# A modulation vector's last eight row chunks, summed by VectorE instead of TensorE

## The chip, the cores and the metric

The kernel runs on one core of a Trainium2 chip. The metric is the device time of one execution in microseconds, lower is better; the times given are medians of several runs. TensorE (PE in the profile) multiplies matrices, VectorE (DVE), ScalarE (ACT) and GpSimd (POOL) work element by element, and SyncE (SP) issues nearly all DMA transfers from one queue.

## The reference

Two transformer-like blocks on 256 tokens of width 2048, all in fp32. What the change touches is the modulation of the first block, and what stands around it:

```python
c_act = jax.nn.silu(c)                          # 1 x 2048
mod = c_act @ w_ada[l] + b_ada[l]               # 2048 x (6 * 2048)
sh1, sc1, gt1, sh2, sc2, gt2 = jnp.split(mod[:, None, :], N_MOD, axis=-1)
h = _rmsnorm(x, norm1_g[l]) * (1.0 + sc1) + sh1
p = h @ w_in[l]
y_rwkv = _rwkv7_mixer(p[..., :N_RWKV_COLS], ...)   # a recurrence over tokens, 16 heads
y_pool = _pool_mixer(p[..., N_RWKV_COLS:], ...)
mix = jnp.concatenate([y_rwkv, y_pool], axis=-1) @ w_out[l]
x = x + gt1 * mix
h = _rmsnorm(x, norm2_g[l]) * (1.0 + sc2) + sh2    # first use of sc2, the fifth vector
x = x + gt2 * _conv_ffn(h, w_up[l], ...)
```

The second block (convolution, windowed attention, gates, another FFN) follows and is not touched.

## The kernel before

**Weights.** All weights stream from HBM in chunks of 1 MB (128 x 2048 fp32) through `raw`, a ring of four slots that SyncE fills strictly in the order `ORDER`, each time when the slot's last reader has signalled (`freed`). A weight chunk ("w") has two halves of 128 x 1024. ScalarE writes a rounded copy `whi` of a half (`cut_hi`, line 1312), VectorE the rest `wlo` (`cut_lo`, line 1773), and TensorE multiplies both with the activations (lines 651 and 652: 128x512 and 128x256). "lead" is the cut of a half some steps ahead of its product; `lo_ready` counts cut halves, `half_used` multiplied ones.

**Modulation.** The six vectors are rows of the product c_act x w_ada. A chunk of w_ada ("ada") is 128 rows by 2048 columns of one vector, 16 chunks to a vector. `ada_chunk` (line 700) multiplies the uncut chunk with `crep`, a column of c_act repeated 32 times, in four column groups that add up in the PSUM bank `ada`; at the end of a vector ScalarE copies the bank to `ada_row` (`copy_ada`, line 1378), TensorE turns it into columns (`ada_turn`, line 709), and VectorE adds the bias into `mod` (`mod_columns`, line 1864). Before, five vectors (`PE_VECTORS`, 80 chunks) go this way: 32 chunks at the start, 6 in the opening segment, and 14 in each of the segments 1 to 3 (`SEGMENT_ADA`), two at each even step below 14. The sixth vector is summed by VectorE row chunk by row chunk in the later up1 stage (`late_row`, line 2221, one instruction for a half of 128 x 1024), and `ada_late` (line 716) sums the 128 partitions with a matrix of ones.

**Segments.** The recurrence of group g (four of them) runs in segment g+1, in 16 steps, mixed by hand with products. In segments 1 to 3 the products are those of the next group's projections; in the last segment (s = 4, here called the last) they are the first half of w_out ("woutp"), one tile of eight pairs of matmuls for each step, in two quarters. `recurrence_step` gives TensorE's small products of a step in two parts: steps 1 to 6 invert matrices (`z_step` line 878, `t_step` lines 891 and 897), steps 7 to 12 pass the state through four chunks (`u_step` 947, `s_step` 958, `r_step` 924, `y_step` 971), step 13 takes the variance (`var_step` 1005) and step 14 spreads it (`var_spread` 1011). Between them lie VectorE's and ScalarE's parts (`recurrence`, lines 1979 to 2049). VectorE's order in a step n of the last segment is: `r_out` in steps 8 and 11, the cut of half n+2, the residual tile of step n-1 (line 2163, two instructions of 128x256), the recurrence part, and at n = 13 `mixed_low` (line 2152). After step 15 it runs

```python
            for s in range(SEGMENTS):
                segment(s)
                if s == SEGMENTS - 1:
                    norm_scale(1, 4, 5, "norm2_g")
            dve.wait_ge(mixed, NGROUP)
            mixed_low(6, 2, NR + 6)
```

and four more cuts. Then comes the stage wout: TensorE's `first_four` makes tiles 0 to 3 in four parts of eight pairs; its parts 0, 1, 2 and 3 each wait for one cut half (those cut in steps 14 and 15 and the first two of the four), and parts 2 and 3 also for `mixed_low(6, 2)`. Twelve tiles of one half each follow, and their residual tiles. A tile of woutp needs the residual tile of three tiles before, one of wout that of four before. The stage ends with the norm of x1, then up1 begins.

**Buffers.** `mix[:, NR:KT]` (the pool mixer's output) is read for the last time in step 0 of the last segment, and `aa` in segment 3.

## Time and profile before

| | us |
|---|---|
| median of 3 runs | 2660.87 |
| lowest, highest | 2657.83, 2666.80 |
| the profiled execution | 2657.71 |
| its span (first to last instruction) | 2655.5 |
| PE busy in the span | 2594.1 |
| DVE busy | 1875.0 |
| ACT busy | 1279.5 |
| DMA moved | 554.86 MB |

Segments 1, 2 and 3 stand at about 213.6, 289.3 and 365.0 us from the start of the span, the last segment at 441.2, the stage wout at 516.0, up1 at 568. A busy PE counts as busy when any matmul is in flight; a wait of an engine stands in brackets behind the instruction that ended it, with the engine, tile and line that released it. Successive instructions of an engine overlap by some hundredths of a microsecond, so that the distance of two starts is a little less than the duration.

### The profile page before, as it was taken

The page shows a single profiled execution, that of the slowest core. Times are in us where ns is not written, and L with a number is a line of the kernel's source. Part 1 is how long each engine was busy: PE and PEld are TensorE (multiplying, and loading weights), DVE is VectorE, ACT ScalarE, POOL GpSimd, SP SyncE. Part 2 cuts the span into 40 slices and gives each one's busy share as a digit, 9 for nine tenths or more (in the row PEclk, how much of TensorE's full clock was granted, in tenths as well). Part 3 has the DMA queues.
Part 4 walks back from the last instruction along what each step waited for, and adds up shares of the span by engine and source line. Part 5 has one row for each costly group of instructions (what it writes and reads, how often), then busy time and mean ns, then how long its engine had stood idle before and what let it go on. Part 6 is the DMA issues. An engine that isn't in the chain of part 4 may idle for free.

```text
span 2655.5 us, 48131 instructions
## 1 busy us (share of the span) xinstructions
PE 2594.1 (98%) x17668; PEld 2176.3 (82%) x17668; DVE 1875.0 (71%) x2718; ACT 1279.5 (48%) x1800; POOL 149.8 (6%) x150
## 2 busy tenths in 40 slices
PE   5999999999999999999999999999999999999998
PEld 1677776888888888888888888888888888888887
DVE  1475666778888887555577877787688888885554
ACT  2354443355555555444433465554455555554443
POOL 1311111020000000000000000001100000000000
PEclk8999999999999999999999999999999999999999
DMA  9957775346666655555555544455555555555553
GB/s 375 381 228 268 290 277 206 139 160 236 237 237 237 237 197 184 205 201 210 199 189 178 188 159 158 160 182 195 190 177 190 189 189 189 190 190 206 205 200 132
DMA packets 86806, 554.86 MB, mean 209 GB/s; under 512 B 8496, under 2 KB 8624, under 8 KB 24496
## 3 DMA queue, kind: packets, MB, share of 16 engines
q1 hardware_dynamic: 86272, 551.78, 56.5%
q8 instruction: 74, 1.21, 0.2%
q10 hardware_dynamic: 432, 1.64, 0.2%
q14 instruction: 28, 0.23, 0.0%
HBM read 551.29 MB, written 2.10 MB: 208 GB/s over the span
## 4 chain that ended last, share of the span: by engine, by line
PE 87%; DVE 6%; DMA 3%; issue 2%; ACT 2%; DVEq 0%; SPq 0%; ACTq 0%
PE bank L651 38%; PE bank L652 19%; PE banks L651 15%; PE banks L652 8%; DMA raw<-in_stream_dram 3%; DVE wlo L1773 2%; PE bank L700 1%; DVE yb L2468 0%; DVE yb L2471 0%; ACT whi L1312 0%; PE banks L878 0%; PE banks L1245 0%; PE banks L1265 0%; PE banks L897 0%; PE banks L1105 0%
## 5 line engine op out<-in xcount | busy, mean ns | idle before, releaser
L1773 DVE TENSOR_TENSOR wlo<-raw,whi 128x1024 fp32r<-128x1024 f32 x846 | 1031.0, 1228 | 213.5 <-ACT whi L1312 209.4
L1312 ACT ACTIVATE whi<-raw 128x1024 fp32r<-128x1024 f32 x846 | 878.4, 1052 | 424.2 <-PE bank L652 325.0
L651 PE MATMUL bank<-act,whi 128*128 128x512 f32 x2928 | 1045.4, 399 | 1.4 <-DVE act L2152 0.9
L652 PE MATMUL bank<-act,wlo 128*128 128x256 f32 x2928 | 819.6, 280 | 0.0
L651 PEld LDWEIGHTS bank<-act,whi 128*128 128x128 f32 x2928 | 548.7, 187 | 146.3 <-issue 18.4
L651 PE MATMUL banks<-act,whi 128*128 128x512 f32 x1792 | 633.9, 396 | 7.9 <-DVE act L1823 6.8
L652 PEld LDWEIGHTS bank<-act,wlo 128*128 128x128 f32 x2928 | 553.2, 189 | 1.0 <-issue 0.7
L652 PE MATMUL banks<-act,wlo 128*128 128x256 f32 x1792 | 504.7, 282 | 0.0
L651 PE MATMUL bank<-ff,whi 128*128 128x512 f32 x1408 | 493.3, 393 | 1.0 <-DVE wlo L1773 1.0
L651 PEld LDWEIGHTS banks<-act,whi 128*128 128x128 f32 x1792 | 338.6, 189 | 91.1 <-issue 13.5
L652 PE MATMUL bank<-ff,wlo 128*128 128x256 f32 x1408 | 392.9, 279 | 0.0
L652 PEld LDWEIGHTS banks<-act,wlo 128*128 128x128 f32 x1792 | 341.8, 191 | 0.0
L651 PEld LDWEIGHTS bank<-ff,whi 128*128 128x128 f32 x1408 | 263.8, 187 | 64.4 <-DVE wlo L1773 1.7
L1599 ACT ACTIVATE yb<-joined,par 128x256 f32<-128x256 f32 x176 | 105.9, 603 | 346.9 <-DVE joined L1793 181.4
L652 PEld LDWEIGHTS bank<-ff,wlo 128*128 128x128 f32 x1408 | 263.8, 187 | 0.0
L2210 DVE SCALAR_TENSOR_TENSOR yb<-joined,par,yb 128x255 f32<-128x255 f32 x352 | 169.1, 481 | 24.7 <-DVE yb L2210 5.5
L2518 POOL TENSOR_TENSOR ssq<-ssq,ft 128x256 f32<-128x256 f32 x75 | 71.0, 947 | 1364.3 <-ACT ft L1585 1345.5
L700 PE MATMUL bank<-raw,crep 128*32 128x512 f32 x640 | 90.1, 665 | 28.8 <-DMA raw<-in_stream_dram 28.8
L651 PE MATMUL bank<-gated,whi 128*128 128x512 f32 x256 | 89.7, 393 | 0.4 <-DVE yb L2468 0.4
L1585 ACT ACTIVATE ft<-x 128x256 f32 (+1 forms) x64 | 26.6, 415 | 106.4 <-DVE x L2162 86.1
L2162 DVE TENSOR_TENSOR x<-bank,x 128x256 f32 (+1 forms) x64 | 27.2, 424 | 70.3 <-PE bank L652 69.2
L700 PEld LDWEIGHTS bank<-raw,crep 128*32 128x32 f32 x640 | 15.6, 113 | 71.6 <-DMA raw<-in_stream_dram 42.9
(281 smaller groups left out, 1943.2 us busy)
## 6 DMA issues: line engine op xcount, KB each, us to landing
raw<-in_stream_dram SPq DMA_DIRECT2D x503, 1024.0 KB, 4.8
late_in<-in_stream_dram SPq DMA_DIRECT2D x16, 1024.0 KB, 6.7
x<-in_x_dram SPq DMA_DIRECT2D x1, 2048.0 KB, 13.6
lora_w<-in_lora_dram SPq DMA_DIRECT2D x1, 1536.0 KB, 12.3
pool_w<-in_pool_w_dram SPq DMA_DIRECT2D x1, 1024.0 KB, 12.1
out_dram<-x SPq DMA_DIRECT2D x2, 512.0 KB, 2.8
out_dram<-x ACTq DMA_DIRECT2D x2, 512.0 KB, 3.0
catt<-in_att_dram ACTq DMA_DIRECT2D x1, 576.0 KB, 3.2
```

What stands on the lines that cost most here:

```text
L651: nc.tensor.matmul(tile_bank(t), wh, flat(pair[:, kt]), start=starts and n == 0, stop=False)
L652: mm = nc.tensor.matmul(small_half(t), wl, pair[:, kt, 0], start=False, stop=stops and last)
L700: mm = nc.tensor.matmul(ada[32 * g:32 * g + 32, :], crep[:, kt], src[:, 512 * g:512 * g + 512], start=kt == 0, stop=kt == KT - 1, tile_pos ...
L1312: nc.scalar.activation(whi[:, k % RING], raw[:, r % RING, 8 * (k % 2):8 * (k % 2) + 8], ACT.Copy)\
L1585: nc.scalar.activation(ft[:, j % 2], one(x, j + 4 * i), ACT.Square).then_inc(sq_ready, 1)
L1599: nc.scalar.activation(yb[:, j], joined[:, j % 2], ACT.Identity, scale=pcol(conv, 3 * j + tap + 12 * i), bias=pcol(bias, j + 4 * i)).then_ ...
L1773: nc.vector.tensor_tensor(wlo[:, k % RING], raw[:, r % RING, 8 * (k % 2):8 * (k % 2) + 8], whi[:, k % RING].bitcast(F32), ALU.subtract).th ...
L2162: return nc.vector.tensor_tensor(dst, half, dst, ALU.add)
L2210: ins = nc.vector.scalar_tensor_tensor(out=yb[:, j, dst], in0=joined[:, j % 2, src], scalar=pcol(conv, 3 * j + tap + 12 * i), in1=yb[:, j, ...
L2518: nc.gpsimd.tensor_tensor(ssq[:], ssq[:], ft[:, q], ALU.add).then_inc(ssq_ready, 1)
```

## The change

Chunks 8 to 15 of the fifth vector (sc2, `VECTORS` index 4) leave TensorE's list: segments 1 and 2 have 12 ada chunks each (none at step 12), segment 3 has 10 (none at steps 10 and 12). The ring has eight entries fewer. The eight chunks come in 16 halves of 512 KB, issued by SyncE between the loads of the last segment into `mix[:, NR:KT]`, two halves at a time; half o waits until VectorE has done half o-2. VectorE scales and adds one half at the end of each of the steps 2 to 15 of the last segment, and the last two in wout at tiles 4 and 5, into `aa`. TensorE sums the partitions at wout's tile 8 (`ada_late`), ScalarE copies before tile 10, TensorE turns at tile 11, and VectorE adds the result to the half vector already in `mod` at tile 12, where `norm_scale` now stands too. ScalarE's copies of the fourth and fifth vectors are at steps 2 and 10 of segment 3 instead of step 12 of segment 2 and step 14 of segment 3.

```diff
-SEGMENT_ADA = 14
+SEGMENT_ADA = {1: 12, 2: 12, 3: 10}
+SEGMENT_FIRST = {1: 38, 2: 50, 3: 62}
+ROWS = 8
+PE_CHUNKS = PE_VECTORS * KT - ROWS
+ROW_STEP = 2
-VECTORS = (1, 0, 2, 3, 4, 5)
+VECTORS = (1, 0, 2, 3, 4, 4, 5)
...
+        row_in = mix[:, NR:KT].rearrange("p (g k) t -> p g (k t)", g=2)
+        row_sum = aa[:].rearrange("p (g k) t -> p g (k t)", g=2)
...
+            def load_row_half(o):
+                q, g = o // 2, o % 2
+                if o == 0:
+                    sp.wait_ge(a_ready, 16 * FILLS.index("mixed") + NR)
+                if o >= 2:
+                    sp.wait_ge(row_added, o - 1)
+                src = stream[KT * 4 + KT - ROWS + q, :, HALF * g:HALF * g + HALF]
+                sp.dma_start(row_in[:, g], src).then_inc(row_full[g], 16)
...
+                behind = n - FIRST_CHUNK["woutp"] - RING
+                if what == "w" and 0 <= behind < ROWS:
+                    load_row_half(2 * behind)
+                    load_row_half(2 * behind + 1)
...
             for n in range(4, TILES["wout"]):
+                if n == 8:
+                    pe.wait_ge(row_added, 2 * ROWS)
+                    pe.wait_ge(tile_sum, FIRST_TILE["wout"])
+                    ada_late(row_sum)
+                if n == 11:
+                    pe.wait_ge(gn_out, NGROUP)
+                    ada_turn(PE_VECTORS)
...
-                    if (s, n) in ((1, 10), (2, 12), (3, 14)):
-                        copy_ada(1 + s)
+                    if (s, n) in ((1, 10), (3, 2), (3, 10)):
+                        copy_ada({(1, 10): 2, (3, 2): 3, (3, 10): 4}[s, n])
...
+                if n == 10:
+                    copy_ada(PE_VECTORS)
...
+            def row_part(o):
+                q, g = o // 2, o % 2
+                dve.wait_ge(row_full[g], 16 * (q + 1))
+                activation = crep[:, KT - ROWS + q, 0:1]
+                if q == 0:
+                    nc.vector.tensor_scalar(row_sum[:, g], row_in[:, g], activation, None, ALU.mult).then_inc(row_added, 1)
+                else:
+                    dve.wait_ge(row_added, o - 1)
+                    nc.vector.scalar_tensor_tensor(out=row_sum[:, g], in0=row_in[:, g], scalar=activation, in1=row_sum[:, g],
+                                                   op0=ALU.mult, op1=ALU.add).then_inc(row_added, 1)
...
-                    elif n == 13:
-                        dve.wait_ge(mixed, NGROUP - 1)
-                        mixed_low(0, 6, NR)
+                    else:
+                        if n == 13:
+                            dve.wait_ge(mixed, NGROUP - 1)
+                            mixed_low(0, 6, NR)
+                        if n >= ROW_STEP:
+                            row_part(n - ROW_STEP)
...
                 segment(s)
-                if s == SEGMENTS - 1:
-                    norm_scale(1, 4, 5, "norm2_g")
...
                 lead("wout", n, 0, 0)
+                if n in (4, 5):
+                    row_part(2 * ROWS - 6 + n)
                 done("wout", n, 0, 0)
                 residual_tile("wout", n, 0, 2)
+                if n == 12:
+                    mod_added(PE_VECTORS)
+                    norm_scale(1, 4, PE_VECTORS + 1, "norm2_g")
```

## Rows read from the trace of the kernel before

**Rows 1.** The page, busy time of each engine in the span.
```profile
PE 2594.1 (98%) x17668; PEld 2176.3 (82%) x17668; DVE 1875.0 (71%) x2718; ACT 1279.5 (48%) x1800; POOL 149.8 (6%) x150
```
**Rows 2.** Busy by stretch: length, busy PE PEld DVE ACT POOL (count), PEclk, DMA share, GB/s.
```profile
365.00:441.20 76.20, 74.90 (x1175) 53.84 (x1174) 48.16 (x85) 31.02 (x53) 8.70 (x6) 1.00 0.72 277
...
458.00:516.00 58.00, 58.00 (x824) 47.57 (x817) 37.65 (x67) 22.70 (x36) 4.11 (x4) 1.00 0.33 111
516.00:528.40 12.40, 11.30 (x67) 9.64 (x65) 8.95 (x14) 4.58 (x6) 0.00 (x0) 1.00 0.67 246
528.40:562.60 34.20, 34.17 (x192) 29.41 (x192) 26.93 (x40) 17.66 (x27) 16.91 (x15) 1.00 0.46 157
```
**Rows 3.** Timeline of PE, end of segment 1: start us, us, instruction, [wait].
```profile
275.63 1.92 PE L700 MATMUL bank<-raw,crep 128*32 128x512 f32 x16
...
283.63 0.66 PE L1011 MATMUL bank<-res,zmat 128*128 128x128 f32 x4 [0.80 <-DVE zmat L2040]
```
**Rows 4.** Timelines of ACT and of DVE in the same stretch.
```profile
277.60 0.63 ACT L1461 ACTIVATE zmat<-t 128x512 f32<-128x512 f32 x1 [6.29 <-DVE t L2035]
278.13 2.18 ACT L1312 ACTIVATE whi<-raw 128x1024 fp32r<-128x1024 f32 x2
...
279.21 2.36 DVE L1773 TENSOR_TENSOR wlo<-raw,whi 128x1024 fp32r<-128x1024 f32 x2 [1.65 <-ACT whi L1312]
...
283.15 0.43 DVE L2040 COPY zmat<-small 128x512 f32<-128x512 f32 x1
```
**Rows 5.** Timelines of PE and of DVE, segment 3, step 10.
```profile
417.72 1.92 PE L700 MATMUL bank<-raw,crep 128*32 128x512 f32 x16
419.58 0.27 PE L958 MATMUL banks<-tok 64*64 64x64 f32 x2
...
417.47 0.41 DVE L2008 COPY us<-banks 64x256 f32<-64x256 f32 x1
420.31 0.48 DVE L2019 SCALAR_TENSOR_TENSOR state<-banks,dc,wssq 128x64 f32<-128x64 f32 x2 [2.43 <-PE banks L958]
```
**Rows 6.** Timeline of ACT, segment 3, step 2; durations of line 1378 (min/median/max ns).
```profile
377.77 0.60 ACT L1440 ACTIVATE tinvt<-banks 128x512 f32<-128x512 f32 x1 [4.95 <-PE banks L891]
...
L1378 ACT ACTIVATE ada_row<-bank x6: 577/590/598, 53.8 to 1061.0; 128x512 f32<-128x512 f32 x6
```
**Rows 7.** Durations (min/median/max ns) of two VectorE lines.
```profile
L2221 DVE SCALAR_TENSOR_TENSOR late_sum<-late_in,crep,late_sum x32: 1276/1280/1281, 619.8 to 958.0; 128x1024 f32<-128x1024 f32 x32
...
L1932 DVE TENSOR_SCALAR yb<-kraw,par x4: 346/353/353, 170.6 to 397.6; 128x256 f32<-128x256 f32 x4
```
**Rows 8.** Timelines of DVE and of PE, last segment, step 9.
```profile
488.99 1.23 DVE L1773 TENSOR_TENSOR wlo<-raw,whi 128x1024 fp32r<-128x1024 f32 x1
490.25 1.00 DVE L2163 SCALAR_TENSOR_TENSOR x<-bank,mod,x 128x256 f32<-128x256 f32 x2
491.17 0.47 DVE L2019 SCALAR_TENSOR_TENSOR state<-banks,dc,wssq 128x64 f32<-128x64 f32 x2
...
491.98 0.34 PE L924 MATMUL banks<-state,ar 64*64 64x64 f32 x8
```
**Rows 9.** Timeline of DVE, from the last segment into wout.
```profile
519.36 4.80 DVE L1773 TENSOR_TENSOR wlo<-raw,whi 128x1024 fp32r<-128x1024 f32 x4
527.33 3.74 DVE L2163 SCALAR_TENSOR_TENSOR x<-banks,mod,x 128x256 f32<-128x256 f32 x8 [3.17 <-PE banks L652]
```
**Rows 10.** Timeline of PE, the turn of the fifth vector.
```profile
461.76 0.60 PE L709 MATMUL bank<-res,ada_row 128*128 128x128 f32 x4
```
**Rows 11.** Timeline of PE at step 1 of the last segment; busy in the stretch behind it.
```profile
453.19 0.69 PE L878 MATMUL banks<-tinvt,bm 64*64 64x64 f32 x32 [2.57 <-DVE tinvt L1995]
...
453.20:458.00 4.80, 4.80 (x104) 4.02 (x104) 3.30 (x5) 1.63 (x2) 1.04 (x1) 0.64 0.23 93
```
**Rows 12.** DMA issues: KB each, median us from issue to landing.
```profile
late_in<-in_stream_dram SPq DMA_DIRECT2D x16, 1024.0 KB, 6.7
...
cw<-in_wkv_dram SPq DMA_DIRECT2D x1, 480.0 KB, 13.9
```

More of the change, by code:

```diff
@@ L74 @@
 OPEN_ADA = {6: 2, 8: 2, 10: 2}
-SEGMENT_ADA = 14
+SEGMENT_ADA = {1: 12, 2: 12, 3: 10}
+SEGMENT_FIRST = {1: 38, 2: 50, 3: 62}
 PE_VECTORS = 5
-LATE = 5
+ROWS = 8
+PE_CHUNKS = PE_VECTORS * KT - ROWS
+ROW_STEP = 2
+LATE = 6
 LATE_FIRST, LATE_END = 2, 2 + KT
@@ L97, in raw_order @@
                 c += 1
-            for _ in range(OPEN_ADA.get(n, 0) if s == 0 else 2 - 2 * (n % 2) if n < SEGMENT_ADA else 0):
+            for _ in range(OPEN_ADA.get(n, 0) if s == 0 else 2 - 2 * (n % 2) if n < SEGMENT_ADA.get(s, 0) else 0):
                 order.append(("ada", a))
                 a += 1
-    assert a == PE_VECTORS * KT
+    assert a == PE_CHUNKS
     return order + [("w", m) for m in range(c, N_WEIGHT_CHUNKS)]
@@ L400, in blocks_program @@
         late_full, late_added = sem("late_full"), sem("late_added")
+        row_full, row_added = [sem(f"row_full{g}") for g in range(2)], sem("row_added")
         sq_ready, ssq_ready, stat_ready, std_ready = sem("sq_ready"), sem("ssq_ready"), sem("stat_ready"), sem("std_ready")
@@ L700, in ada_chunk @@
                     mm = nc.tensor.matmul(ada[32 * g:32 * g + 32, :], crep[:, kt], src[:, 512 * g:512 * g + 512],
-                                          start=kt == 0, stop=kt == KT - 1, tile_position=(0, 32 * g))
+                                          start=kt == 0, stop=kt == KT - 1 or n == PE_CHUNKS - 1, tile_position=(0, 32 * g))
                 mm.then_inc(ada_used, 1)
@@ L710, in ada_turn, with ada_late @@
                 mm.then_inc(ada_turned, 1)
-            def ada_late():
-                pe.wait_ge(late_added, 2 * KT + 2)
+            def ada_late(total):
                 for g in range(4):
                     mm = nc.tensor.matmul(ada[32 * g:32 * g + 32, :], ones[:, 0:32],
-                                          late_sum[:, g // 2, 512 * (g % 2):512 * (g % 2) + 512], start=True, stop=True,
+                                          total[:, g // 2, 512 * (g % 2):512 * (g % 2) + 512], start=True, stop=True,
                                           tile_position=(0, 32 * g))
@@ L1147, in segment @@
                             quarter(s, q)
-                        if part == 1 and n % 2 == 0 and n < SEGMENT_ADA and not last:
+                        if part == 1 and n % 2 == 0 and n < SEGMENT_ADA.get(s, 0):
                             for a in (n, n + 1):
-                                ada_chunk(ADA0 + sum(OPEN_ADA.values()) + SEGMENT_ADA * (s - 1) + a)
+                                ada_chunk(SEGMENT_FIRST[s] + a)
                         if not last:
@@ L1201, in _ @@
             loop("up1", 4, LATE_END, None, LATE_FIRST)
-            ada_late()
+            pe.wait_ge(late_added, 2 * KT + 2)
+            ada_late(late_sum)
             loop("up1", 4, 22, None, LATE_END)
@@ L1372, in copy_ada @@
             def copy_ada(n):
-                act.wait_ge(ada_used, KT * (n + 1) if n < PE_VECTORS else KT * PE_VECTORS + 1)
+                act.wait_ge(ada_used, KT * (n + 1) if n < PE_VECTORS - 1 else PE_CHUNKS + n - PE_VECTORS + 1)
                 if n:
@@ L1864, in mod_columns, with mod_added @@
                 nc.vector.tensor_tensor(dst, src, bias, ALU.add).then_inc(mod_ready, 1)
+            def mod_added(n):
+                dve.wait_ge(ada_turned, n + 1)
+                dve.wait_ge(mod_ready, n)
+                src = aux[:, :].rearrange("p (b g r) -> p g b r", b=4, g=4)[:, :, :, 0]
+                dst = mod[:, VECTORS[n]].rearrange("p (g b) -> p g b", g=4)
+                nc.vector.tensor_tensor(dst, src, dst, ALU.add).then_inc(mod_ready, 1)
+            def row_part(o):
[8 more added lines that the diff above has]
+                                                   op0=ALU.mult, op1=ALU.add).then_inc(row_added, 1)
             def norm_scale(n, which, ready, name):
@@ L2335, in _ @@
             mod_columns(LATE)
-            dve.wait_ge(mod_ready, 6)
+            dve.wait_ge(mod_ready, LATE + 1)
             dve.wait_ge(derived, 6)
```

## The prediction

> **What bounds the kernel now.** I read the page first. TensorE is busy for 98% of the span, VectorE for 71% [rows 1]. So time can come back only where TensorE does less, and only if nothing else was the last to finish there. Then I took the busy time by stretch, because that share is an average over stages [rows 2]. In segment 3 TensorE works 74.90 of 76.20 us. In steps 2 to 14 of the last segment it works 58.00 of 58.00, while VectorE works 37.65 and has 20.35 us free. At the step into wout (516.0 to 528.4) VectorE has 3.4 us free, nearly all of it one wait of 3.17 us at the end [rows 9]. The reader should see that VectorE's free time in the last segment is about as large as the work that the change puts there, and that it lies in pieces between things TensorE waits for. The timelines of these places give the rest.
>
> **What TensorE gives up.** A pair of ada chunks takes 1.92 us, and the next instruction starts 1.86 us behind its start [rows 3, 5]. Four pairs go: 7.4 us of TensorE time. What each is worth is read at its place.
>
> *Step 12 of segments 1, 2 and 3 (three pairs).* At the end of segment 1 TensorE waits 0.80 us for VectorE's zmat, at 283.63 [rows 3]. I follow that wait back [rows 4]: zmat 283.15, which needed ScalarE's square root, which stands on ScalarE behind a tile that VectorE joined after two cuts (279.21, 2.36 us), which waited for ScalarE's cuts (278.13), which stand behind the square at 277.60, which waited for VectorE's y_out. VectorE came to y_out through its own queue. No link is the pair at 275.63. Without the pair TensorE reaches its next quarter 1.86 us sooner and then waits: about 0.9 us in front of the variance products (the square ends at 278.23) and 1.65 us at 283.63 in place of 0.80. Worth zero, three times over. The bound on the other side is the full 3 x 1.86 = 5.6 us.
>
> *Step 10 of segment 3 (one pair).* Here the pair is on the path [rows 5]. VectorE's u_out ends at 417.88, the state products could start at 417.95 and start at 419.58, and VectorE waits 2.43 us for them. All that follows up to the last segment hangs on them. Worth 1.63 us.
>
> *The copies that move.* The first chunk of the fifth vector waits for the fourth vector's copy (0.59 us), now at step 2 of segment 3. ScalarE has been idle 4.95 us before its instruction at 377.77 [rows 6], so the copy is done by about 373.5. TensorE comes to that chunk at 378.1. It costs nothing. If that cover were gone it would cost 0.6. Later weight chunks only arrive sooner, with eight chunks fewer ahead of them.
>
> **What VectorE takes on.** The sixth vector's rows are the same instruction on the same shape: 1.28 us [rows 7]. Successive starts lie closer than durations: four cuts of 1.22 us take 4.80 [rows 9]. I take 1.20 for a part and keep 1.28 as upper bound. The two first parts are TENSOR_SCALAR, 0.35 us at a quarter of the size [rows 7]; four of them (1.4) bound one from above, 0.7 is my value. Both fall in steps where VectorE has over 2 us free, so it doesn't matter. I lay the parts into VectorE's order, step by step, with its durations of before, and let each instruction start when its engine and its releaser allow. Without the parts this hand replay gives the starts of before within 0.1 us. Clock times below are those of before, with no shift for segment 3.
>
> 1. Steps 2 to 8: VectorE is caught up each time before TensorE needs it. Nothing.
> 2. Step 9 [rows 8]: before, the cut starts at 488.99 and the state output at 491.17, and TensorE's r products at 491.98. A part of 1.20 now stands in front of the cut, and the state output ends at 492.84. TensorE starts at 492.89: 0.94 us late.
> 3. Step 10: the part of step 9, cut (1.20), residual (0.92) and u_out end at 497.31. TensorE, already 0.94 late, waits 0.38 more.
> 4. Step 12: the same queue makes y_out end at 507.30 and the square at 507.97. TensorE waits 0.35 more.
> 5. Steps 13 to 16: `mixed_low` (1.67), the part, a cut, a residual tile, the group's scaling, then 1.1 us on ScalarE, two finishing operations, the part of step 14, and only then the cut that `first_four`'s part 1 needs: done at 521.89, wanted at 520.49. 1.45 late.
> 6. Residual tile, the part of step 15, residual tile, `mixed_low(6, 2)` and the next cut end at 526.78. `first_four`'s part 2 wants it at 524.75. 2.08 late. Before, this cut was the first of the four that began at 519.36 [rows 9], ready 1.1 us ahead.
>
> Sum of waits: 0.94 + 0.38 + 0.35 + 1.45 + 2.08 = 5.20 us. The 3.17 us in which VectorE waited afterwards [rows 9] don't help, as they lie behind the wait. The last two parts, in wout, are hidden: VectorE has 7.3 us free there [rows 2], and tile 8 needs the sum only after about 10 us.
>
> **What TensorE takes on.** `ada_late` for the rows is one group of eight, half a pair: 0.93 us. The extra turn is 0.60 us, 0.53 from start to start [rows 10]. Both stand in wout, where TensorE is busy 34.17 of 34.20 us [rows 2], so both count: 1.46 us. The copy (0.59), the bias-like addition and the moved `norm_scale` (0.17 each) have most of a tile (2.8 us) to spare.
>
> **Transfers.** Half o is issued when half o-2 has been added, two steps (about 9 us) ahead of its use. The nearest row is late_in: 1 MB lands in 6.7 us [rows 12], and these are 512 KB, with DMA busy 0.33 there [rows 2]. Hidden. SyncE's waits hold back the weights queued behind them: chunk 5+b of the last segment is issued at the end of step 2b+1 and first cut at step 2b+7. Also hidden.
>
> **Sum.** -1.63 + 5.20 + 0.93 + 0.53 = +5.0 us. With 1.28 for a part the waits grow to 5.76 and the sum is +5.6. With 0.80, far below any such row, it is +2.5. With the three other pairs worth all of their 5.6 us it would be -0.6. Against the profiled execution (2657.71, span 2655.5) this is 2662.7. That execution lies 3.2 us under the median of the runs shown, so against the median it is 2665.9. I predict 2666. A measurement of this kernel tells a change from none at about 0.3%, 8 us: this reads as no change, a little on the slow side.
>
> **Rivals.**
>
> *Everything comes back.* VectorE's order leaves room for the parts and the three pairs of step 12 are worth their time: -7.4 + 1.46 = -5.9, 2655. For it speaks 20.35 us of free time for 14 parts of 1.20 [rows 2]. Against it, the chain in rows 4, in which TensorE has no part. Even this stays inside 8 us. Chance 0.06, half of it with something on top.
>
> *The parts fit, the pairs don't pay.* -1.63 + 1.46 = -0.2, 2660.7. This needs VectorE to be off the path at steps 9 to 16. Chance 0.09.
>
> *The clock falls (slower).* Behind a wait of 2.57 us in step 1 of the last segment TensorE's granted clock is 0.64 on average over 4.80 us, so it fell to its lower level (1.2 GHz) for part of it: 4.80 x 0.36 = 1.7 us lost [rows 11]. The change makes such places: 1.45 and 2.08 us close together at wout's start, and 0.9 and 1.65 us at each of three segment ends. One fall makes +6.7, four make 5.0 + 6.9 = +11.9, 2673. From two falls on it decides against "no change". For it: the waits are many, and 2.57 was enough. Against it: each is shorter than 2.57, and the wait of 1.10 us at 528.39, the same kind, was followed by a clock of 1.00 [rows 2]. Chance 0.19 for two or more.
> The Trainium skill, TensorE: Matmul & The Clock Gate, section "A second HAM failure mode: psum-queue depth-cycling", says that frequent short idles between groups of matmuls can make the clock swing between its levels. By that rule the time would be nearer the +11.9 of this rival; by the clock of 1.00 behind the single short wait it stays at the sum.
>
> *Row halves land late (slower).* If a half took 13.9 us like the small transfer in rows 12, then the two steps of 9.1 us would stretch by 4.8, six times: +29 on top. That one was issued with larger ones around it. It decides from landings of about 9 us. Chance 0.04.
>
> **How the numbers follow.** The forecast, +2.5 to +8 and thus 2663 to 2669, has 0.62. The range must hold the rivals down to the pairs' price and up to four falls, and the spread of the runs shown (2657.8 to 2666.8), so 2657 to 2673. Faster by over 0.3%: 0.03. Slower by over 0.3%: the clock 0.18, late halves 0.04 and 0.02 of the forecast's upper edge, 0.24. Within: 0.73.
>
> **What would show each step.** In the changed profile: (a) at the ends of segments 1 to 3 the wait at line 1011 is about 1.65 us, with another near 0.9 in front of line 1005, and segments 1 and 2 are as long as before (75.7 us). Shorter ones make the zero wrong. (b) Segment 3 is 1.6 us shorter. (c) TensorE waits for VectorE's state at steps 9 and 10, and twice within `first_four`, 1.5 and 2.1 us. If VectorE shows idle time in steps 9 to 16 other than for ScalarE's 1.1 us, my order is wrong. (d) The parts last 1.28 us and wait for no DMA. (e) Granted clock of 1.00 from 516 to 562. (f) From 441 to the norm of x1, 6.7 us more than before. The forecast fails if (e) shows 0.9 or less, or if the waits in (c) are absent.

## The result and the profile after

The changed kernel takes 2669.15 us in the median of 18 runs (2664.63 to 2673.71), the kernel before 2660.26 in 18 runs beside them (2654.83 to 2666.8). The ratio is 1.003, 95% interval 1.0022 to 1.0038: slower by 8 us (5.9 to 10.1), just at the bound of what I had called no change, inside the range and 3 us above the forecast. The profiled execution of after is the slowest of its 18 runs (2673.71, 4.6 above the median) and that of before was 2.5 below its own. So the two traces differ by 15.6 us of span where the medians differ by 8.9, and what is read from them must be split into what the program does and what an execution draws. The sections below do that.

The page of the changed kernel, busy time by engine. Against [rows 1] VectorE's sum is 17.6 us up, as it should be; TensorE's is 7.3 up too, though it has four pairs less: its work took longer somewhere.

```profile
span 2671.1 us, 48070 instructions
PE 2601.4 (97%) x17616; PEld 2176.5 (81%) x17616; DVE 1892.6 (71%) x2735; ACT 1278.5 (48%) x1801; POOL 150.7 (6%) x150
```

The waits of TensorE in the changed kernel from 170 to 600 us: line, releaser, sum in us, times, longest.

```profile
PE bank L1026 <- ACT zmat L1491: 3.2, 4, 1.0
PE bank L1032 <- DVE zmat L2092: 2.9, 3, 1.4
PE banks L899 <- DVE tinvt L2047: 2.5, 1, 2.5
PE banks L673 <- DVE wlo L1805: 2.4, 2, 1.7
...
PE banks L899 <- issue: 1.7, 1, 1.7
...
PE banks L945 <- DVE state L2071: 1.6, 4, 1.1
```

**The pairs of step 12.** The timeline of TensorE at the end of segment 1, where [rows 3] stood before. The pair is gone; TensorE comes to the variance products early and waits 0.97 us, then waits 1.40 in place of 0.80:

```profile
278.00 1.05 PE L1026 MATMUL bank<-res,zmat 128*128 128x2 f32 x8 [0.97 <-ACT zmat L1491]
...
283.33 0.66 PE L1032 MATMUL bank<-res,zmat 128*128 128x128 f32 x4 [1.40 <-DVE zmat L2092]
```

Segment 1's products begin 0.26 us earlier than before and those of segment 3 0.14 earlier: two pairs of 1.86 us went out of segments 1 and 2 and nothing came back.

**The pair of step 10 of segment 3.** The product ahead of it (L968, 420.06) is 3.30 late, for a reason that follows. The state products start at 421.48, 1.90 after those of before [rows 5], so 1.40 us came back; for 0.39 of the rest TensorE waits for VectorE:

```profile
420.06 0.45 PE L968 MATMUL banks<-rs,tinv 64*64 64x64 f32 x8
...
421.48 0.27 PE L979 MATMUL banks<-tok 64*64 64x64 f32 x2 [0.39 <-DVE us L2060]
```

**A stall that nobody forecast.** In step 4 of segment 3 the 32 small products of the inverse break off after 17. The timeline of TensorE, and the busy time around it (columns as in [rows 2]):

```profile
390.71 0.50 PE L899 MATMUL banks<-tinvt,bm 64*64 64x64 f32 x17
...
392.88 0.46 PE L899 MATMUL banks<-tinvt,bm 64*64 64x64 f32 x15 [1.67 <-issue]
```

```profile
386.00:391.00 5.00, 5.00 (x121) 3.05 (x112) 1.06 (x3) 2.10 (x4) 2.79 (x2) 1.00 0.59 221
391.00:394.00 3.00, 1.33 (x31) 1.08 (x24) 0.60 (x1) 0.00 (x0) 0.00 (x0) 0.93 0.89 322
394.00:397.00 3.00, 3.00 (x50) 2.37 (x52) 1.22 (x2) 0.97 (x1) 0.00 (x0) 0.50 0.88 369
397.00:400.00 3.00, 3.00 (x73) 2.46 (x69) 2.00 (x3) 1.77 (x5) 0.00 (x0) 1.00 0.20 27
```

"Issue" means that no semaphore released the instruction. TensorE stands 1.67 us in the middle of a group that waits for nothing, and behind it the granted clock is 0.50 (the 1.2 GHz level) for 3 us. Together 3.4 us: the work before it is 0.14 us ahead of before's, the work behind it 3.30 late. In before all of 391 to 397 is busy at a clock of 1.00. The low clock is this execution's: the profiles of runs 1, 2, 4, 7 and 8 have nine more such idles of 0.21 to 1.80 us, and behind none of them does the clock fall.

**The last segment and wout.** TensorE's timeline at step 9, step 10, the variance products and the two parts of `first_four`, where [rows 8, 9] stood:

```profile
495.26 0.34 PE L945 MATMUL banks<-state,ar 64*64 64x64 f32 x8 [1.11 <-DVE state L2071]
...
499.88 0.27 PE L979 MATMUL banks<-tok 64*64 64x64 f32 x2 [0.47 <-DVE us L2060]
...
510.59 1.05 PE L1026 MATMUL bank<-res,zmat 128*128 128x2 f32 x8 [0.27 <-ACT zmat L1491]
...
524.18 0.51 PE L673 MATMUL banks<-act,whi 128*128 128x512 f32 x1 [0.74 <-DVE wlo L1805]
...
528.93 0.50 PE L673 MATMUL banks<-act,whi 128*128 128x512 f32 x1 [1.66 <-DVE wlo L1805]
```

Five waits at the five forecast places, for the forecast releasers, 4.25 us in all. The wait of 1.10 us at wout's fifth tile (528.39 in the kernel before) is in both kernels and not among them. The parts and the transfers of the row halves (duration in ns min/median/max, first and last start):

```profile
L588 SPq DMA_DIRECT2D mix<-in_stream_dram x16: 327/328/435, 447.5 to 526.3; - x16
L1915 DVE SCALAR_TENSOR_TENSOR aa<-mix,crep,aa x12: 1274/1277/1286, 473.1 to 525.0; 128x1024 f32<-128x1024 f32 x12
L1912 DVE TENSOR_SCALAR aa<-mix,crep x2: 743/744/746, 462.8 to 468.3; 128x1024 f32<-128x1024 f32 x2
...
DMA to landing us min/median/max: 3.5/4.4/6.4
```

### The profile page after: what moved, and what is told of

It reads as the page before. It is cut to its first block, busy times and chain, and to the rows that moved or that the text cites. A ratio compares the mean times of both kernels' runs of the same rounds, so it can differ in the third digit from the quotient of the medians.

```text
span 2671.1 us, 48070 instructions
## 1 busy us (share of the span) xinstructions
PE 2601.4 (97%) x17616; PEld 2176.5 (81%) x17616; DVE 1892.6 (71%) x2735; ACT 1278.5 (48%) x1801; POOL 150.7 (6%) x150
## 4 chain that ended last, share of the span: by engine, by line
PE 87%; DVE 7%; DMA 3%; issue 2%; ACT 1%; DVEq 0%; SPq 0%; ACTq 0%
PE bank L673 38%; PE bank L674 19%; PE banks L673 16%; PE banks L674 8%; DMA raw<-in_stream_dram 3%; DVE wlo L1805 2%; PE bank L722 2%; DVE yb L2526 0%; DVE yb L2529 0%; PE banks L899 0%; ACT whi L1342 0%; DVE aa L1915 0%; DVE x L2218 0%; PE banks L1275 0%; PE banks L1295 0%
## 5 line engine op out<-in xcount | busy, mean ns | idle before, releaser
L722 PE MATMUL bank<-raw,crep 128*32 128x512 f32 x576 | 83.3, 679 | 26.9 <-DMA raw<-in_stream_dram 26.9
L1822 DVE TENSOR_REDUCE joined<-banks 128x256 f32<-128x512 f32 x50 | 34.3, 691 | 56.7 <-PE banks L674 56.6
```

What stands on the lines that cost most here:

```text
L722: mm = nc.tensor.matmul(ada[32 * g:32 * g + 32, :], crep[:, kt], src[:, 512 * g:512 * g + 512], start=kt == 0, stop=kt == KT - 1 or n == P ...
L1822: nc.vector.tensor_reduce(dst, halves, AX.X, ALU.add).then_inc(tile_sum, 1)
```

## The experiments

All are timed in five rounds beside the kernel before. "Late" and "early" below are starts of the same instruction against the kernel before, counted from segment 1's products, so that the start of an execution, which varies by some 2 us, is left out. One thing in these offsets is not of the programs: the clock behind the wait in step 1 of the last segment fell in the kernel before [rows 11], which cost it 1.5 us, and whether it falls there differs between executions of one program (last section).

**1. The removal alone.** The changed kernel without row transfers, parts, late sum and turn: 72 chunks on TensorE, so half of the fifth vector is missing from the sum.

```
-                    load_row_half(2 * behind)
-                    load_row_half(2 * behind + 1)
...
-                    pe.wait_ge(row_added, 2 * ROWS)
...
-                    ada_late(row_sum)
...
-                    ada_turn(PE_VECTORS)
...
-                        if n >= ROW_STEP:
-                            row_part(n - ROW_STEP)
...
-                    mod_added(PE_VECTORS)
```

> Leaves the last eight chunks of the fifth vector out altogether (no transfers, no parts, no late sum, no second turn), so sc2 lacks half of its sum. My theory: only the pair at step 10 of segment 3 was on TensorE's path, so the time is 1.4 to 1.6 us under the kernel before, unless the stall of 3.3 us that the changed kernel's profile shows in step 4 of segment 3 (1.67 us with no releaser, then a low clock) belongs to the shorter TensorE program: then it is 1.7 us over it, and the stall is in this profile too. Rival (everything comes back): 7.4 us under it, with no wait at lines 1005 and 1011 beyond the old 0.80 us.

2661.76, ratio 1.0006 (0.9993 to 1.002). Four pairs, 7.4 us of TensorE's work, are gone and the kernel isn't faster. Segments 1 and 2 are as long as before; step 10 gives 1.4; and the same 17 and 15 split is there, with a second one in step 5:

```profile
392.85 0.46 PE L898 MATMUL banks<-tinvt,bm 64*64 64x64 f32 x15 [1.41 <-issue]
...
400.03 0.27 PE L898 MATMUL banks<-tinvt,bm 64*64 64x64 f32 x2 [1.80 <-issue]
```

They cost 3.75 us, so segment 3 ends 2.3 us late. Step 1 of the last segment gives back 1.5 of that, because the clock stayed at 1.00 there, and the stage wout 0.6. The norm of x1 is 0.2 late. By the program the stalls took more than the pairs gave. The stall therefore doesn't come from the parts or their transfers.

**2. The parts cut to 16 columns.** All transfers, waits and the late sum stay; only VectorE's time goes; the sum leaves out the other columns.

```
-  nc.vector.scalar_tensor_tensor(out=row_sum[:, g], in0=row_in[:, g], ...
+  nc.vector.scalar_tensor_tensor(out=row_sum[:, g, 0:16], in0=row_in[:, g, 0:16], ...
```

> The changed kernel with all its transfers, waits and TensorE work, but each part of VectorE works on 16 columns in place of 1024 (sc2 lacks the rest). My theory: the four waits of TensorE for VectorE's queue (1.1, 0.5, 0.3 in steps 9 to 13 and 0.7 and 1.7 at wout's start, some 4.3 us) go, and the time falls by 4 to 5 us from the changed kernel. Rival (late transfers or the SyncE queue hold things up): the waits stay. Rival (the loss lies outside these stages): it falls by less than 2 us. The TensorE program is that of the changed kernel, so a stall in step 4 of segment 3 that comes from its length shows here again; one that comes by chance most likely does not.

2665.01, 1.0017 (1.0003 to 1.0031). The five waits are gone; the stall (1.68, and a second one of 1.00 in step 5, 3.2 us lost with the clock at 1.00) and the late sum with its turn remain; the norm of x1 is 2.9 late. The transfers as such cost nothing.

**3. The parts alone.** The kernel before plus the 16 transfers and the 16 parts, whose sum is not used; TensorE's program is that of before.

```
+                if what == "w" and 0 <= behind < ROWS:
+                    load_row_half(2 * behind)
+                    load_row_half(2 * behind + 1)
...
+                        if n >= ROW_STEP:
+                            row_part(n - ROW_STEP)
```

> The kernel before with only the 16 transfers of 512 KB and VectorE's 16 parts added at the places of the change; TensorE still multiplies all 80 chunks and the sum of the parts is not used. My theory: 4.5 to 5.8 us over the kernel before, all of it in steps 9 to 13 and at wout's start. Rival (VectorE's free time holds them): within 1 us of it. If a slower up1 loop comes with the parts' transfers or code, it shows here as more than 6 us; if it comes with the TensorE program, this one has the loop of before (22.19 us an iteration).

2663.12, 1.002 (1.0005 to 1.0035). TensorE's waits from 440 to 570 us in this kernel:

```profile
PE banks L670 <- DVE wlo L1792: 3.0, 3, 1.9
...
PE banks L943 <- DVE state L2050: 1.1, 1, 1.1
...
PE banks L977 <- DVE us L2039: 0.5, 1, 0.5
PE bank L1024 <- ACT zmat L1480: 0.2, 1, 0.2
```

4.8 us of waits, the norm of x1 6.5 late, and no stall in segment 3. This is the parts' cost by itself. The lateness grows by more than each wait: by 1.19, 0.88, 0.51, 1.07, 2.20 and 0.56 us at waits of 1.12, 0.45, 0.25, 0.74, 1.93 and 0.35.

**4. The changed kernel again.**

> The changed kernel again, for a second profile. If the 3.3 us stall in step 4 of segment 3 and the up1 loop of 22.61 us an iteration (22.19 before) are properties of its program, both stand here again, and the time is 8 to 9 us over the kernel before. If they vary from execution to execution, the stall is elsewhere or absent and the loop differs, while the waits in steps 9 to 13 and at wout's start stand within 0.1 us.

2670.52, 1.0034 (1.002 to 1.0047). Stall of 1.68 at the same instruction, waits 0.27, 0.74 and 1.71, the norm of x1 8.3 late (9.3 in the first profile). The first profile shows one stall and a low clock behind it; this one shows two stalls and a clock of 1.00 from 391 to 400, and loses 2.9 us there in place of 3.4:

```profile
398.09 0.27 PE L899 MATMUL banks<-tinvt,bm 64*64 64x64 f32 x2 [0.72 <-issue]
```

**5. Other pairs.** Which pair is dropped should matter more than how many. The parts stay; the pairs of steps 2, 4, 6 and 10 of segment 3 go, those of step 12 come back, and ScalarE's copies stand where they stood in the kernel before.

```
-SEGMENT_ADA = {1: 12, 2: 12, 3: 10}
+SEGMENT_ADA = {1: (0, 2, 4, 6, 8, 10, 12), 2: (0, 2, 4, 6, 8, 10, 12), 3: (0, 8, 12)}
```

> The changed kernel with other pairs of ada chunks taken from TensorE: segments 1 and 2 keep all seven pairs (step 12 again too), segment 3 keeps only those of steps 0, 8 and 12, so the pairs of steps 2, 4, 6 and 10 go. Still 72 chunks, the parts on VectorE are unchanged, and the copies of the third and fourth vector go back to where they were. Theory 1 (a pair is worth what TensorE's place on the path makes it worth; step 12 is free, the others are not): segments 1 and 2 as long as before; in segment 3 three more pairs are worth 1.4 to 1.86 us each, so 4.2 to 5.6 us less than the changed kernel, 2664 to 2665. Rival (pairs at other steps are hidden as well, VectorE or ScalarE being last): less than 1 us less than the changed kernel. The stall in segment 3 (1.4 to 1.7 us with a lower clock behind it) and the loop with 0.3533 us for a pair of matmuls: if they hang on the place in TensorE's program, the loop is slow again, because it begins at the same place in the program as in the changed kernel, and the stall, if it comes, comes at another instruction.

2663.78, 1.0012 (0.9999 to 1.0024). Segments 1 and 2 as before; in segment 3 steps 4, 6 and 10 give 1.45, 1.95 and 1.40, and step 2 gives 1.43 that is lost again one step on, where TensorE now waits for ScalarE. TensorE's timeline there:

```profile
384.33 0.69 PE L899 MATMUL banks<-tinvt,bm 64*64 64x64 f32 x32 [1.79 <-ACT tinvt L1470]
```

Together 4.8 us, and no stall anywhere. The norm of x1 is 0.7 late against 9.3 and 8.3 in the changed kernel; 1.5 of the difference is the clock in step 1 of the last segment, which stayed at 1.00 here and fell in both of those. By the ratios (1.0012 against 1.003) the kernel gained 4.8.

**6. Moved parts.** On top of 5: no part in steps 8 to 13.

```
+ROW_PARTS = {2: 2, 3: 2, 4: 1, 5: 1, 6: 1, 7: 1}      # then 1 in step 14, 2 behind the four cuts
-                if n in (4, 5):
+                if n in (4, 5, 8, 9, 10):              # tiles of wout
```

> As e5_other_pairs, and the parts on VectorE stand elsewhere: two each at the ends of steps 2 and 3, one each at the ends of steps 4 to 7, one between the scaling and the finishing of the last group in step 14, two behind the four cuts at the start of wout, five in wout's tiles 4, 5, 8, 9 and 10; the sum goes to TensorE at tile 12 and its turn at tile 14. Theory 1 (the parts cost only what they put in front of something TensorE waits for, and these places are free): the waits of 1.1 and 0.5 us at steps 9 and 10, 0.3 in front of the variance and 0.7 and 1.7 in first_four go; 4.3 to 5.2 us less than e5_other_pairs, about 2660. Rival (VectorE has no true slack, the delay comes back elsewhere, or the halves' transfers land late when two parts follow each other): less than 1.5 us less than e5_other_pairs, or waits for a DMA at the end of step 3.

2666.71, 1.0015 (0.9999 to 1.0031): a miss. The waits at steps 9 to 13 and in `first_four` are gone, and others came. VectorE's timeline in step 3 of this kernel, and TensorE's waits from 440 to 570 us:

```profile
463.87 1.28 DVE L1917 SCALAR_TENSOR_TENSOR aa<-mix,crep,aa 128x1024 f32<-128x1024 f32 x1 [0.87 <-DMA mix<-in_stream_dram]
```

```profile
PE banks L912 <- DVE zmat L2053: 1.7, 1, 1.7
...
PE bank L737 <- DVE aa L1917: 1.6, 1, 1.6
...
PE banks L673 <- DVE wlo L1805: 0.3, 1, 0.3
```

The second part of step 3 waited for a transfer that could only start when the half two before it had been added; 1.8 us of the last segment went there and 1.0 in front of the state products at 481.6. Another 1.1 us is not of the arrangement: in segment 3 the clock fell behind TensorE's wait of 1.80 us for ScalarE, the one of 1.79 that left it at 1.00 in run 5. The three parts in a row in tiles 8 to 10 took 1.76 us each, not 1.28, and the late sum waited 1.58 for them.

**7. TensorE's program restored.** The stall stood in every profile of the changed kernel's TensorE program (the changed kernel twice, runs 1 and 2), and neither with that of before nor with the other pairs of runs 5 and 6. Is it the place of the instructions? The changed kernel with harmless small matmuls put where TensorE idles.

```
             for n in range(KT):
                 ada_chunk(n)
+                if n == 1:
+                    for _ in range(16):
+                        nc.tensor.matmul(work[0][0:32, 0:16], ones[:, 0:32], ones[:, 0:16], ...)
...
             stat("x1")
+            ...             # four waits already met, and seven such matmuls into ada
             spread_norm("x1")
```

> The changed kernel with harmless instructions added to TensorE's program, so that each instruction from segment 3 on stands about where it stood in the program before: 16 matmuls of 16 columns behind the second ada chunk, where TensorE waits 5.4 us for a transfer, and 7 of them and four waits that are already met behind the sums of the norm of x1, where it waits for the norm. Nothing else is changed. Theory 1 (the stall in step 4 of segment 3 and the slower first loop of up1 hang on where the instructions stand in the program): the stall of 1.7 us and the low clock behind it are gone, minus 3.3 us, and the loop takes 338.2 us from its first late row to its last in place of 344.7, minus 6.5 to 7, the second loop gives back 1.7; about 8 us less than the changed kernel, 2661. Rival (they come from the changed work itself, its transfers or its timing): stall and loop as in the changed kernel, time within 1.5 us of it.

2665.91, 1.0017 (1.0004 to 1.003). The group in step 4 is whole again:

```profile
391.85 0.69 PE L903 MATMUL banks<-tinvt,bm 64*64 64x64 f32 x32
```

but 0.31 us appeared in segment 1, where 1.3 us were lost in all, and 1.20 at another instruction of segment 3:

```profile
423.63 0.50 PE L673 MATMUL bank<-act,whi 128*128 128x512 f32 x1 [1.20 <-issue]
```

So in this program's one profile the stalls stand elsewhere. The norm of x1 is 7.6 late, 1.7 better than the changed kernel, the median 3 better; the expected 8 was not reached.

**8. The program before, shifted.** The same 16 matmuls in the kernel before.

> The kernel before with 16 matmuls of 16 columns added behind the second ada chunk, where TensorE waits 5.4 us for a transfer; all that follows stands 16 fp32 matmuls further on in TensorE's program. No other work is changed. Theory 1 (the place in the program alone costs or gives time): the up1 loop is slow (about 344.7 us from first to last late row) or another length, or a stall without a releaser shows somewhere in the segments, although not one instruction of theirs is changed; plus 3 to 9 us if both come. Rival (the program's place has no effect): offsets to the kernel before stay within 0.5 us everywhere, time within 1.5 us.

2661.09, 1.0001 (0.9988 to 1.0015). One stall of 0.21 us and 0.9 us lost in two places of the segments, nothing in the total. A shift alone need not cost.

**9. Parts spread.** On top of 5, no two parts in a row before step 14 and every second tile in wout.

```
+ROW_AHEAD = (3, 4)              # before the inverse's work
+ROW_PARTS = (1, 2, 4, 5, 6, 7)  # at the end; then 1 in step 14, 2 behind the four cuts
+                if n in (4, 6, 8, 10, 12):             # tiles of wout; late sum at 14, turn at 15
```

> e6_moved_parts, with the parts where VectorE was seen idle in it: one each at the ends of steps 1, 2, 4, 5, 6 and 7, one each in front of the inverse's work in steps 3 and 4, one in step 14, two behind the four cuts, and one in every second tile of wout (4 to 12). Two parts never follow each other before step 14, so that a half has 4.4 us and more to land. The sum goes to TensorE at tile 14, the turn at tile 15. Theory 1 (what e6_moved_parts lost was its own arrangement: 1.8 us behind the double part of step 3 that waited 0.87 us for its transfer, 1 us behind the next one, 1.6 us at the sum and 0.35 at a cut): no wait of TensorE for a part is left; from the last segment's step 1 to the norm of x1 it takes 4.5 to 5 us less than e6_moved_parts, and the norm of x1 begins about 3 us before that of the kernel before. Up1's slower first loop is still there (+6.4, the next loop -1.7). So about +1.5 against the kernel before in its profile, 2661 to 2662. Rival (VectorE has no more room in the last segment): waits of over 2 us in all appear elsewhere between steps 1 and 16, and the time stays at 2665 or above.

2659.0, 0.9995 (0.9986 to 1.0005). Of the waits at steps 9 to 13 and in `first_four` none is left; TensorE waits 0.59 us for the parts before the late sum. The norm of x1 begins 4.2 us early, 1.5 of it by the clock that did not fall in step 1 of the last segment. The mechanism of the forecast works in both directions.

**10. Parts spread, program restored.** The same with 23 small matmuls in the two waits of the norm of x1, 7 of them and four waits already met behind its sums and 16 behind its spreading.

> e9_parts_spread, with 23 harmless matmuls of 16 columns and four waits that are already met added to TensorE's program, 7 behind the sums of the norm of x1 and 16 behind its spreading, where TensorE waits 0.55 and 1.86 us, so that the up1 loops begin where they begin in the kernel before. Theory 1 (the loop's pace hangs on its place in the program): first late row to last in 338.2 us in place of 344.7, the loop behind it 1.7 slower, so 4.7 to 5 us less than e9_parts_spread; about 2656.5, faster than the kernel before by 0.1 to 0.2%. If the matmuls in the wait also keep the granted clock up, the first six pairs of up1 take 0.35 us each in place of 0.64: another 1.5 to 1.8 us less. Rival (the pace comes from the timing of the transfers): the loop stays at 344.7 us, time within 1.5 us of e9_parts_spread.

2655.62, 0.9987 (0.9975 to 1.0): the lowest ratio of all, 3.5 us ahead of the kernel before at the edge of what can be measured, and not to be told from run 9 (0.9986 to 1.0005).

**11. The kernel before, padded.** 24 small matmuls in the two waits of that norm.

> The kernel before with 24 harmless matmuls of 16 columns in the two waits of the norm of x1 (0.6 and 1.9 us) and nothing else changed. Theory 1 on the clock (TensorE's idle 1.9 us in front of up1 is why the first six pairs of up1 take 0.64 us): with work in the wait they take 0.35 us, 1.5 to 1.8 us less. Rival: no change of those pairs. Theory 1 on the place (what stands behind them stands 24 fp32 matmuls further on): the up1 loop may have another length than 338.2 us; the place of e8_before_shifted, 16 further on, left it fast, those of the changed kernel, 24 and 32 less, made it slow, so this run adds one point. Rival (the place has no part in it): 338.2 us.

2660.27, 1.0004 (0.9992 to 1.0017). TensorE now waits 0.50 where it waited 1.86, and the pairs behind it still take 0.64 us. A wait filled with small matmuls did not keep the clock up here; in run 10, four slow pairs in place of some nine.

**12. Run 9 again.** Runs 7 and 10 had the up1 loop at before's pace and seemed to prove that the pace hangs on the program's place. Run 9 had it too, without restored places.

> e9_parts_spread once more, unchanged. It had the fast first up1 loop although that loop begins at the same place in TensorE's program as in the changed kernel. Theory 1 (the pace of a long stretch belongs to the program, though not to the place of its first instruction alone): 332.9 us from the first to the last issue of a late row again, the next loop fast again, and a time within 1.5 us of 2659. Rival (it is drawn anew in each execution): 339.2 us, as in the other kernels with the shortened program, or another pace in the second loop or in the stretch behind down1.

2659.99, 0.9991 (0.9977 to 1.0004). The busy time of 640 to 940 us and 990 to 1050 us, first in run 9 and then in this one; TensorE never waits in either, and the number to read is its count of matmuls:

```profile
640.00:940.00 300.00, 300.00 (x1732) 262.26 (x1731) 258.10 (x353) 158.27 (x218) 0.00 (x0) 1.00 0.63 235
990.00:1050.00 60.00, 60.00 (x348) 52.46 (x347) 45.27 (x66) 32.15 (x44) 0.00 (x0) 1.00 0.53 191
```

```profile
640.00:940.00 300.00, 300.00 (x1700) 260.21 (x1700) 253.83 (x346) 154.74 (x214) 0.00 (x0) 1.00 0.62 231
990.00:1050.00 60.00, 60.00 (x342) 52.05 (x341) 43.85 (x64) 30.96 (x43) 0.00 (x0) 1.00 0.51 182
```

The same program ran the loop at both paces: the theory of run 7 on the loop falls in its strict form. A draw of an execution is worth 6.4 us there. The norm of x1 is only 1.0 us early here; the 3.1 us between the two runs lie in steps 1 to 3 of the last segment, behind a wait that both have (last section).

## Why the prediction was right, point by point

**The pairs of step 12** (forecast 0). Right: waits of 0.97 and 1.40 in segment 1 where I had said 0.9 and 1.65, the same within 0.05 in segment 3, and in segment 2 0.97 and then 0.20, because the clock was low between the two (see below). What stands behind each of the three ends is within 0.2 us of where it was with the pair, and run 5, which puts the pairs back, is as long in segments 1 and 2. The step of the argument that carried it was following the wait through ScalarE and VectorE until no link was TensorE.

**The pair of step 10** (forecast -1.63). Right; it measured -1.40 in the changed kernel and -1.40 again in run 5.

**The five waits** (forecast 5.20). Right in places and releasers; 4.25 in size: 1.11, 0.47, 0.27, 0.74 and 1.66 against 0.94, 0.38, 0.35, 1.45 and 2.08. `first_four` was over-sized by 1.1. Run 2 takes them away together with VectorE's time, run 3 brings them without anything else. The sum took the waits alone; what follows a wait comes later by more than the wait, because the first matmul behind it takes 0.50 and the next 0.40. Counted as lateness the five are 1.17, 0.54, 0.50, 1.06 and 1.96, together 5.2 us. That this meets the forecast 5.20 is luck: two errors, waits too long and no restart, cancel.

**Late sum and turn** (forecast 1.46). Right: the matmul behind the sum starts 0.99 after it, that behind the turn 0.35 after it, 1.34 in all; as lateness, with the restarts behind them, 1.17 and 0.46.

**Transfers** (forecast 0). Right: landing in 4.4 us, at most 6.4, and no part waited. Run 6 shows the edge: two parts in a row and one waits 0.87.

**The rival of the clock** (0.19). It had two kinds of places. In `first_four` it did not occur: from 520.3 to 533.0, over both waits, the granted clock is 1.00.

```profile
520.30:533.00 12.70, 10.30 (x57) 8.45 (x56) 11.80 (x14) 5.58 (x7) 0.00 (x0) 1.00 0.75 267
```

At the segment ends it did occur, which I had not looked for. Behind the wait of 0.97 us at 353.64 in segment 2 the clock is low for 3.4 us, and the wait before the spread shrinks from 1.40 to 0.20:

```profile
356.00:359.50 3.50, 3.31 (x13) 2.51 (x12) 2.73 (x6) 0.67 (x2) 0.00 (x0) 0.51 0.44 115
```

```profile
358.98 0.88 PE L1032 MATMUL bank<-res,zmat 128*128 128x128 f32 x4 [0.20 <-DVE zmat L2092]
```

The five profiles without the pairs of step 12 (the changed kernel twice, runs 1, 2 and 7) show it at six of their fifteen segment ends, the nine others at none. Each time it cost at most 0.2 us, because the lost time was time that TensorE would have waited at the spread. So the rival was right that such waits can bring the clock down and wrong in its price of 1.7 us: it had not asked what stands behind them. The clock also fell behind the stall of 1.67 us, about as long as the wait of 1.66 that left it alone. The Trainium skill, TensorE: Matmul & The Clock Gate, section "A second HAM failure mode: psum-queue depth-cycling", has the clock swing when short idles come often; the trace doesn't bear that out for the five waits of the last segment and wout.

**What was missing** is a term, not a step that failed: the stall, 3.4 us in the changed kernel's first profile and 2.9 in its second, at the same instruction in all four profiles of this TensorE program (the changed kernel twice, runs 1 and 2; in three of them with a second one in step 5). Measured terms, the waits and the late sum as lateness: -1.40 + 5.2 + 1.6 + 3.4 = 8.8 of the 9.3 that the profile shows to the norm of x1 (8.3 in run 4); the medians say 8.0 (5.9 to 10.1). Without the stall the terms make 5.4, and 5.0 was forecast. Of the signs that I had named, (b), a segment 3 shorter by 1.6 us, failed by it: that segment is 2.0 longer. That the stall's 3 us still lie within the range is luck: its upper end was there for falls of the clock. Behind the norm the first profile shows another +6.6. Of these +5 are the paces of the up1 loops (+6.4 and -1.7), which run 12 shows to differ between executions of one program; 1.5 lie between 1300 and 1800 us and are not explained.

What TensorE waited for can be read from the transfers, though no run moved it by itself. Behind 60 us the fourteen profiles show ten idles for "issue" of more than 0.15 us, and in all ten TensorE goes on 2.2 to 2.4 us after a packet of the queue of instructions has started: 390.66 and 392.88 in the changed kernel, 397.80 and 400.03 in run 1, 421.25 and 423.63 in run 7. In segment 3 such packets come 3 to 22 us apart, so this is hardly chance: TensorE was waiting for instructions. The transfers of 380.5 to 389.4 us, in the changed kernel and then in the kernel before (queue, packets, MB, share):

```profile
q1 hardware_dynamic: 351, 2.61, 71.7%
```

```profile
q1 hardware_dynamic: 346, 2.57, 76.3%
q8 instruction: 1, 0.02, 0.7%
```

The queue of instructions brings a packet at 379.8 and the next at 390.7 in the changed kernel; the kernel before has one more at 386.0. All four profiles with the stall have that gap of 10.6 to 10.9 us, and in the ten others none there is longer than 9.5. The length alone doesn't decide: gaps of 12 to 16 us that begin between 401 and 412 are in all fourteen profiles, and only in run 7 does TensorE stand at the end of one. Nor was the late packet seen to stand behind more weights, as their queue was busy for 71.7% in the gap against 76.3% in before. The Trainium skill, Advanced Engine Details and Errata, section "ISA Cache", says that instructions come in lines of 16 KB, 256 of them; the packets of 0.02 MB agree, and by that rule taking instructions out shifts where a line ends. Why one packet is late in one program and not in another stays open, and so does whether a restored program changes the odds of the loops' pace: the slow first loop came in seven of eight profiles of unrestored shortened programs and in none of the six others, but the medians, which agree with the account to the norm of x1, leave it a microsecond or so by my estimate.

## What to carry to other kernels

Removed work is worth what the last wait behind it allows: three of the four pairs gave nothing, while those of steps 4 and 6, of the same kind and 30 us away, gave 3.4 us. Free time on an engine has to be found piece by piece, between what others wait for: 16 parts in the same VectorE cost 6.5 us in a row of steps and 0.6 where it was seen idle (run 9). And a gain of a few us that rests on one profile against another must be looked for in the medians too, since an undisturbed loop alone can differ by 6 us between two executions of one program.

## What was not expected of the hardware

- A long stretch of matmuls in which TensorE never waits, at a granted clock of 1.00, runs at one of two paces and keeps it to its end: a pair of 512 and 256 columns every 0.3467 or 0.3533 us. The two come in executions of the same program (run 9 and run 12).
- The clock behind one and the same wait of 2.6 us in step 1 of the last segment also differs between executions: it stayed at 1.00 in six of the fourteen profiles. Windows of 4.8 us behind it, in run 9 and in run 12; before it was 0.64 [rows 11]:

```profile
447.20:452.00 4.80, 4.05 (x108) 3.47 (x109) 3.75 (x6) 1.65 (x3) 1.30 (x2) 1.00 0.44 171
```

```profile
448.50:453.30 4.80, 4.80 (x80) 3.93 (x72) 3.96 (x6) 1.63 (x2) 0.01 (x1) 0.50 0.31 84
```

- A part takes 1.28 us in the last segment and 1.76 in wout, where GpSimd adds squares of the norm. Timelines of VectorE and of GpSimd in the changed kernel:

```profile
539.99 1.76 DVE L1915 SCALAR_TENSOR_TENSOR aa<-mix,crep,aa 128x1024 f32<-128x1024 f32 x1
...
543.71 1.76 DVE L1915 SCALAR_TENSOR_TENSOR aa<-mix,crep,aa 128x1024 f32<-128x1024 f32 x1
```

```profile
538.25 0.74 POOL L2576 TENSOR_TENSOR ssq<-ssq,ft 128x256 f32<-128x256 f32 x1 [0.18 <-ACT ft L1615]
539.16 1.51 POOL L2576 TENSOR_TENSOR ssq<-ssq,ft 128x256 f32<-128x256 f32 x1 [0.17 <-ACT ft L1615]
543.20 1.20 POOL L2576 TENSOR_TENSOR ssq<-ssq,ft 128x256 f32<-128x256 f32 x1 [2.53 <-ACT ft L1615]
```

GpSimd's addition is 0.74 where VectorE runs no cut or part at its start, and 1.20 or 1.51 where a cut runs then; the part that comes next takes 1.76, so both sides pay. The Trainium skill, SBUF — State Buffer, section "Who interferes with whom", says that a VectorE instruction with two SBUF inputs and a reading GpSimd instruction exclude each other; an extra 0.48 and 0.46 us on the two sides agrees with taking turns. For the two parts of the changed kernel this was hidden; for the three in a row of run 6 it was not: three times 0.48 us against the late sum's wait of 1.58.
